# One register load at the entry to the expert loop, and another running order of the experts

## The reference

```python
logits = t @ w_router + b_router             # 256 tokens, 32 experts
top_val, top_idx = lax.top_k(logits, 4)      # four experts for each token
gate_w = softmax(top_val)
# for every expert e, on the tokens that chose it:
hb = xb @ w_exp_in[e] + b_exp_in[e]          # 1024 -> 2048
g = minimum(hb[:, :1024], 7.0); u = clip(hb[:, 1024:], -7.0, 7.0)
a = g * sigmoid(1.702 * g) * (u + 1.0)
y = a @ w_exp_out[e] + b_exp_out[e]          # 1024 -> 1024
# out[token] = sum over its four experts of gate * y, then a residual and a layer norm
```

## Time and profile before

| | us |
|---|---|
| median of 3 runs | 1500.67 (1499.29 to 1502.35) |
| profiled execution, its own time | 1501.61 |
| its span in the trace | 1499.7 |
| TensorE matmul busy | 1336.8 (89%) |
| VectorE, ScalarE, GpSimd busy | 449.4, 359.7, 139.4 |
| data moved | 494.37 MB, mean 330 GB/s over the span |

### The profile page before, as it was taken

The page is one execution under the profiler, slowest core; times in us unless marked ns, Lnnn a source line. Parts: engine busy times, 40 slices in busy tenths (PEclk is TensorE's granted clock), DMA queues, the critical chain, the costliest instruction groups (busy, mean ns, idle before and its releaser), DMA issues.

```text
span 1499.7 us, 25549 instructions
## 1 busy us (share of the span) xinstructions
PE 1336.8 (89%) x9369; PEld 800.7 (53%) x9370; DVE 449.4 (30%) x910; ACT 359.7 (24%) x691; POOL 139.4 (9%) x65
## 2 busy tenths in 40 slices
PE   7999999998999999779998888988879988889965
PEld 6455999987989854334343333343433434333432
DVE  1326687745543871111111111111111111111112
ACT  1234666545566521000000100010010001000101
POOL 0000112005766400000000000000000000000000
PEclk9999999999999999899999999999999999999997
DMA  9441466855344569989999999999999999999996
GB/s 340 149 137 56 112 187 190 322 192 192 134 152 169 184 285 426 406 355 425 428 427 424 428 427 427 423 427 427 427 424 427 427 425 426 428 427 425 422 427 249
DMA packets 113494, 494.37 MB, mean 330 GB/s; under 512 B 7617, under 2 KB 55089, under 8 KB 80465
## 3 DMA queue, kind: packets, MB, share of 16 engines
q1 hardware_dynamic: 111971, 491.50, 81.5%
q10 hardware_dynamic: 1486, 2.34, 0.4%
HBM read 492.76 MB, written 1.06 MB: 329 GB/s over the span
## 4 chain that ended last, share of the span: by engine, by line
PE 63%; DMA 27%; issue 4%; DVE 3%; ACT 3%; SPq 0%; DVEq 0%; ACTq 0%
DMA big_mem<-in_w_exp_in 25%; PE ps L983 17%; PE ps L1025 7%; PE ps L703 5%; PE ps L705 5%; PE ps L704 5%; PE ps L531 4%; PE ps L966 4%; PE ps L675 2%; DMA big_mem<-in_w_exp_out 2%; PE ps L727 1%; PE ps L728 1%; PE ps L729 1%; PE ps L1048 1%; PE ps L1039 1%
## 5 line engine op out<-in xcount | busy, mean ns | idle before, releaser
L983 PE MATMUL ps<-big_mem,ring_mem 128*32 128x512 f32 (+1 forms) x2304 | 373.3, 623 | 54.8 <-DMA big_mem<-in_w_exp_in 54.7
L983 PEld LDWEIGHTS ps<-big_mem,ring_mem 128*32 128x32 f32 (+1 forms) x2304 | 112.5, 122 | 292.9 <-issue 198.7
L1025 PE MATMUL ps<-big_mem,x 128*32 128x256 f32 (+1 forms) x1888 | 186.6, 438 | 5.2 <-ACT x L1596 3.3
L703 PE MATMUL ps<-hT_hi,w_hi 128*128 128x256 f32 x600 | 171.1, 285 | 1.3 <-DVE hT_lo L1683 1.3
L705 PE MATMUL ps<-hT_hi,w_lo 128*128 128x256 f32 x600 | 169.8, 283 | 0.0
L704 PE MATMUL ps<-hT_lo,w_hi 128*128 128x256 f32 x600 | 169.7, 283 | 0.0
L966 PEld LDWEIGHTS ps<-ring_mem,h 128*128 128x128 f32 x1024 | 132.8, 199 | 61.0 <-issue 61.0
L966 PE MATMUL ps<-ring_mem,h 128*128 128x96 f32 x1024 | 150.1, 290 | 0.0
L2169 DVE TENSOR_SCALAR ring_mem<-ps 128x256 f32<-128x256 f32 (+1 forms) x36 | 18.7, 520 | 413.3 <-PE ps L983 413.3
L1583 ACT ACTIVATE ring_mem<-ring_mem 128x256 f32<-128x256 f32 (+1 forms) x36 | 17.7, 493 | 479.6 <-DVE ring_mem L2169 479.6
L1025 PEld LDWEIGHTS ps<-big_mem,x 128*32 128x32 f32 (+1 forms) x1888 | 72.1, 117 | 105.9 <-issue 69.0
(11 more groups left out here) (347 smaller groups left out, 1495.7 us busy)
## 6 DMA issues: line engine op xcount, KB each, us to landing
big_mem<-in_w_exp_in SPq DMA_DIRECT2D x128, 2048.0 KB, 21.2
big_mem<-in_w_exp_out SPq DMA_DIRECT2D x128, 1024.0 KB, 20.8
ring_mem<-in_w_in SPq DMA_DIRECT2D x15, 2048.0 KB, 8.0
ring_mem<-in_w_up SPq DMA_DIRECT2D x44, 512.0 KB, 4.8
ring_mem<-in_w_down SPq DMA_DIRECT2D x5, 2048.0 KB, 8.5
ring_mem<-in_w_out SPq DMA_DIRECT2D x4, 2048.0 KB, 8.4
ring_mem<-in_w_branch_a SPq DMA_DIRECT2D x1, 2048.0 KB, 7.7
ring_mem<-in_w_branch_b SPq DMA_DIRECT2D x1, 2048.0 KB, 7.4
```

Source lines behind the costliest of these rows:

```text
L703: mm(out, hi, x_hi, start=start, stop=False)
L983: last = mm(out, stationary, weights[:, f, w * q:w * (q + 1)] if m > XS else weights[:, :, w * q:w * (q + 1)], start=start, stop=stop)
L1025: last = mm(ps[m * q:m * (q + 1), 4 + at // XS, 0:w], aT[:, k % n, k // n, :], wout[:, k, w * q:w * (q + 1)], start=(k == 0), stop=(k == K ...
```

## The change

Four edits:

1. TensorE: the two products that count tokens go from between the gather's halves to directly behind the rank products; the filler of 512 columns becomes one of 256.
2. TensorE: `counts_ready` is waited for, and the first value of `further` loaded, ahead of the wait for the gates and their transpose. The second value isn't loaded but set to 0; it is loaded only when the first pass outside the loop wasn't taken.
3. VectorE: `own` for expert 0 is made before the residual, `pos` directly behind `further` and ahead of the gates.
4. The table: places 2 and 3 get the ranks 29 and 28 (after 31 and 30 at places 0 and 1), and the remaining 28 places a spread with step 23 modulo 28 in place of step 13 modulo 30.

```diff
-    stay[:, RANKS:RANKS + 2] = E - 1, E - 2
-    stay[:, RANKS + 2:RANKS + E] = 13 * (np.arange(E - 2)[None, :] + 26) % (E - 2)
+    stay[:, RANKS:RANKS + 4] = E - 1, E - 2, E - 3, E - 4
+    stay[:, RANKS + 4:RANKS + E] = 23 * (np.arange(E - 4)[None, :] + 26) % (E - 4)
...
             mm(ps[:, 5, E:2 * E], tri, sel[:, 1, :], start=False, stop=True).then_inc(s["rank_ps"], 1)
-            keep_busy(1, 7)
+            mm(ps[:, 4, 0:E], ones, sel[:, 0, :], start=True, stop=False)
+            mm(ps[:, 4, 0:E], ones, sel[:, 1, :], start=False, stop=True).then_inc(s["rank_ps"], 1)
+            mm(ps[:, 7, 0:SEQ], ident, stay[:, 0:SEQ], start=True, stop=True)
...
                 else:
-                    mm(ps[:, 4, 0:E], ones, sel[:, 0, :], start=True, stop=False)
-                    mm(ps[:, 4, 0:E], ones, sel[:, 1, :], start=False, stop=True).then_inc(s["rank_ps"], 1)
                     pe.wait_ge(s["picks_ready"], 1)
...
+            extra_reg, more_reg, next_extra, next_more = (pe.alloc_register("pe_" + z) for z in ("extra", "more", "next_extra", "next_more"))
+            pe.wait_ge(s["counts_ready"], 1)
+            pe.reg_mov(extra_reg, pe.value_load(further[0:1, 0, 0:1], min_val=0, max_val=TRIO - 1))
+            pe.reg_mov(more_reg, 0)
             pe.wait_ge(s["gates_done"], 1)
             nc.tensor.transpose(ps[0:2 * E, 6, GATE_AT:GATE_AT + P], gate_pair[:], ident).then_inc(s["gateT_ps"], 1)
-            pe.wait_ge(s["counts_ready"], 1)
...
-            pe.reg_mov(extra_reg, pe.value_load(further[0:1, 0, 0:1], min_val=0, max_val=TRIO - 1))
-            pe.reg_mov(more_reg, pe.value_load(further[0:1, 1, 0:1], min_val=0, max_val=PASSES - 1))
...
                 one_pass(GROUPS[1], 16, load_next)
                 turn_end()
+            with pe.If_eq(nth_reg, 0):
+                pe.reg_mov(more_reg, pe.value_load(further[0:1, 1, 0:1], min_val=0, max_val=PASSES - 1))
             with pe.Fori(0, MOST_PASSES):
...
+            dve.wait_ge(s["c_lo_b"], 4)
+            own_row(0, 0)
             dve.wait_ge(s["const_ready"], 1)
...
             v.tensor_copy(further[:], cnt[:]).then_inc(s["counts_ready"], 1)
+            link(v.scalar_tensor_tensor(pos[:], ps[:, 5, 0:T * E].rearrange("p (t e) -> p t e", t=T), 1.0, sel[:], ALU.add, ALU.mult))
             dve.wait_ge(s["own_act"], 3)
```

More of the change, by code:

```diff
@@ L1106, in one_pass @@
                 pe.reg_add(turn_reg, turn_reg, 1)
-            extra_reg, more_reg, next_extra, next_more = (pe.alloc_register("pe_" + z) for z in ("extra", "more", "next_extra", "next_more"))
-            pe.reg_mov(extra_reg, pe.value_load(further[0:1, 0, 0:1], min_val=0, max_val=TRIO - 1))
-            pe.reg_mov(more_reg, pe.value_load(further[0:1, 1, 0:1], min_val=0, max_val=PASSES - 1))
             nth_reg, place_reg, landed_reg, step, step_landed = (pe.alloc_register("pe_" + z) for z in ("nth", "place", "landed", "step", "step_landed"))
@@ L2064, in shifted1, with own_row @@
                 return v.scalar_tensor_tensor(h1[:, t, :], h1[:, t, :], bn[:, 16 * t + 13:16 * t + 14], bc[:, 1, :], ALU.mult, ALU.add)
+            def own_row(e, p):
+                v.tensor_scalar(own, stay[:, bass.ds(OWN + e, 1)].broadcast_to([P, 2 * XS]), 0.0, None, ALU.is_equal).then_inc(s["own_ready"], 1)
+            dve.wait_ge(s["c_lo_b"], 4)
+            own_row(0, 0)
             dve.wait_ge(s["const_ready"], 1)
@@ L2138, in _ @@
             v.memset(posb[:, :, E:E + 1, :], -1.0)
-            link(v.scalar_tensor_tensor(pos[:], ps[:, 5, 0:T * E].rearrange("p (t e) -> p t e", t=T), 1.0, sel[:], ALU.add, ALU.mult))
             link(v.tensor_scalar(posb[:, :, 0:E, 0], pos[:], -1.0, None, ALU.add))
@@ L2176, in swiglu @@
                 v.tensor_tensor(a, u, sig, ALU.mult).then_inc(s["a_ready"], 1)
-            def own_row(e, p):
-                v.tensor_scalar(own, stay[:, bass.ds(OWN + e, 1)].broadcast_to([P, 2 * XS]), 0.0, None, ALU.is_equal).then_inc(s["own_ready"], 1)
             def output(at, m):
@@ L2189, in _ @@
                 dve.reg_mov(r, 0)
-            own_row(0, 0)
             for p in range(1, PASSES):
```

## The result

The changed kernel takes **1515.34 us** (median of 4 runs, 1514.15 to 1515.60) against 1501.51 (1499.29 to 1502.54) for the kernel before on the same chip: ratio 1.0093, 95% interval 1.0075 to 1.011. It is slower, by 14 us where 10 were forecast. The profiled execution took 1515.60 us with a span of 1513.7 (before 1501.61 and 1499.7).

What follows compares the result with a forecast made beforehand. The weight stream's start, holes and short tail were taken to bound the kernel. -4.1 - 7.5 + 20.8 + 1 = +10.2 us on 1500.67 gave 1511 us, range 1504 to 1525.

Steps and rivals of the forecast that it cites:

- What bounds the kernel: Expert part: the DMA weight stream sets the end, through its start, its holes and a short tail; 29.5 us per place.
- Entry, -2.5: Ahead of pass 0: earlier counts and one register load under the gather start pass 0 at 547.9, 2.5 us sooner.
- Clock, -1.6: Pass 0: the shorter gap ahead of it removes TensorE's half-clock stretch, saving 1.6 us, bounds 0 to -1.7.
- first issue: SyncE's first weight transfer for place 1: moves from 556.15 to 552.0, -4.1 us for the whole stream.
- Early holes, -7.5: Stream from 590 to 680 us: light passes at places 2 and 3 close the holes there, -7.5 us.
- Each jump pays: Rival, chance 0.27: ends of places 2 and 3 also pay 7.35 us each, giving 1524 us.
- No second fetch: Rival, chance 0.11: the second code fetch, behind place 4, isn't there; -4.7 us, giving 1506.
- Place 6, hole 8.3: Behind heavy place 6: it starts 16.4 us late, less the 8.1 tolerated, a hole of 8.3 us.
- Places 11, 17 and 28: 2.0, 8.5, 2.0: Behind the other heavy places: holes of 2.0, 8.5 and 2.0 us; place 17 includes 4.9 for the output bias.
- Low clock at places 10 and 27, +1: Middle passes behind light ones, at places 10 and 27: low-clock stretches at times, 1 us added.
- The tail: After the last byte: two light passes, then the norm, the same as before.
- The rule: Heavy passes with a light one behind: 8.1 us late is tolerated; each microsecond beyond is a hole in the stream.

Runs made afterwards that it cites:

- heavy pair: Order with one light place ahead of each heavy one, its heavy expert of place 20 exchanged with the light one of place 14: 1506.81 us.

## Why the prediction was right, and which term was mis-sized

The time was in the range and on the forecast side. Step by step:

- **What bounds the kernel.** Right. From the last landing to the end of the span it is 16.9 us before, 16.4 after, 16.2 with the entry alone and with light places ahead: the time follows the last landing, and that follows the holes. Over all kernels run this tail is 15.1 to 16.9 us, with the same code in it, so differences in time below 2 us between kernels aren't safely those of the holes.
- **Entry, -2.5.** Measured -2.7 (1.40 us from the transpose to pass 0; the forecast had 1.43). The 1.40 is no fixed price behind the transpose, though: with a middle pass at place 3, whose gather has the low stretch, the transpose runs 7.12 us behind the first rank product, 1.5 more than in the changed kernel (5.61), and pass 0 only 0.3 more (7.32 against 7.01). What stands ahead of pass 0 is the sequencer's own chain: the load at 544.57, then register moves up to the branch of L1143 at 546.74.
- **Clock, -1.6.** From the start of pass 0 to the first issue it took 5.83 us and takes 4.16: -1.67. Right here, but not as firm as a single value sounds: with the new table in the old kernel the low stretch there is 6.8 us long, and that distance 6.74 us.
- **Early holes, -7.5.** Measured -6.1 (7.1 to 1.0). The 7.5 were read off the sum of the stretches and all put down to late issues. Only the 5.3 us at place 4 were that (the issue at 653.11). The hole at place 2 is of another kind and stayed (0.7 before, 1.0 now). All its transfers were issued 9.7 us or more before they landed. The fourth quarter of `w_exp_in` landed 5.9 us behind the third in place of 4.9 (599.36 to 605.26), in the stretch that also holds the first long branch and its three instruction packets. It measures 2.1 with the entry alone and 2.0 with two light places ahead. Why the transfer takes longer there isn't shown.
- **Each jump pays (the first rival, 0.27).** Rejected: L1154 is long once in 31, its median 210 ns, though places 2 and 3 took the same jump.
- **No second fetch (0.11).** Rejected: 5.89 us at 681.6, behind place 4 as forecast.
- **Place 6, hole 8.3: the mis-sized term.** It measures **12.9**. Place 5 started 15.3 us late (forecast 14.8), as it should. Pass 5 then took 689.50 to 724.75, 35.25 us, where the forecast had 31 (29.5 and 1.6). So place 6 was 21.0 late, not 16.4, and 21.0 - 8.1 is the hole. The 4.1 us are the clock. Two stretches of the changed kernel's pass 5 (granted clock third from the right):

```profile
688.60:695.40 6.80, 5.90 (x16) 2.10 (x18) 0.00 (x0) 0.00 (x0) 0.00 (x0) 0.50 0.98 407
712.50:715.90 3.40, 3.40 (x10) 0.99 (x10) 0.00 (x0) 0.00 (x0) 0.00 (x0) 0.50 0.97 414
```

The only low stretch of that pass in the kernel with the bias moved, which has the same code and order up to there:

```profile
689.80:693.20 3.40, 2.77 (x10) 1.21 (x12) 0.00 (x0) 0.00 (x0) 0.00 (x0) 0.50 1.00 414
```

9.3 us of busy time at half the clock here, 2.8 there, where the same pass took 31.94 us; 3.1 with the new table in the old kernel, where it took 32.11. Half of 9.3 - 2.8 is 3.25, and the passes differ by 3.3. Half of 9.3 is 4.65, so at full clock this pass would have taken 30.6. The first 5.9 us came directly behind the 5.4 us in which TensorE stood idle for the fetch. The other 3.4 lie 23 us further on, behind gaps of 0.63, 0.47 and 0.24 us that the kernel with the bias moved has as well, without a low stretch: that the fetch caused them isn't shown. The prediction knew of this: the earlier trace rows has a first product of 1.07 us behind the first fetch, and the rival with more fetches carried a low clock. The forecast itself had none behind the second.
- **Places 11, 17 and 28: 2.0, 8.5, 2.0.** Measured 1.8, 9.5, 1.8. Place 17 was 17.6 late, forecast 10.1 + 1.6 + 4.9 = 16.6. All three terms were a little off. The middle pass starts the next one 9.8 late. The second one loses 0.9, not 1.6 (the middle pass of place 22, behind another middle one, takes 30.4 us): the prediction took 3.4 us at half the clock off its 32.7, but that stretch of the kernel before lasts to 615.3, 4.4 us into the pass. The bias adds 5.2 (35.6 against 30.4). Together 15.9, which is what the kernel with a middle pass at place 3 measures. The 1.7 that bring it to 17.6 are the low clock, at place 15.
- **Low clock at places 10 and 27, +1.** Nothing of it is seen there: both heavies behind them are exactly 10.0 late. It fell in place 15, so that place 16 started 11.5 late, where it is 9.8 with the bias moved:

```profile
1012.90:1016.30 3.40, 3.40 (x8) 0.97 (x10) 0.00 (x0) 0.00 (x0) 0.00 (x0) 0.50 0.98 419
```

- **The tail.** 16.4 us from the last byte to the end, 16.9 before.

In all: -4.9 (first issue) - 6.1 + 26.0 = +15.0 for the last landing, which moved by 14.5. The 0.5 between them are small differences in the rate, below what I can assign. The span grew by 14.0 us where 10.2 were forecast. Place 6 alone was 4.6 under, the early holes 1.4 and place 17 1.0. The low-clock term of 1, the first issue (0.8 better than forecast), the two small holes (0.4), the tail and the rate (0.5 each) went the other way. The total is nearer than its largest term, and that much of it is luck.

**The rule holds**: hole = lateness of the heavy pass less 8.1. Over the kernels run, in order of places:

| kernel | lateness of a heavy place | hole behind it |
|---|---|---|
| changed | 21.0, 10.0, 17.6, 10.0 | 12.9, 1.8, 9.5, 1.8 |
| order only | 18.4, 9.9, 17.6, 10.0 | 10.3, 1.9, 10.0, 2.0 |
| bias moved | 17.9, 10.0, 12.6, 9.9 | 9.8, 2.0, 4.5, 1.7 |
| middle at place 3 | 9.9, 11.7, 15.9, 10.0 | 1.8, 3.7, 7.8, 1.9 |
| light ahead | 9.0 (place 6) | 1.1 |
| heavy pair | 8.9 (place 6), 23.1 (place 14) | 2.5, 15.2 |
| heavy at place 2 | 20.1 (place 2) | 13.2 |
| entry only, two light ahead | 8.1 and less | none |

Two of these are off by more than 0.4 us, the first of the heavy pair (2.5 where 0.8 is due) and the one at place 2 (13.2 where 12.0 is due). Both heavy passes began at the low clock, and took 47.3 and 48.1 us instead of 45.8: the 8.1 are for a heavy pass at full clock. With the 1.5 and 2.3 us more of these passes 2.3 and 14.3 are due. At place 2 the slow transfer of that place took 1.1 of them, as a hole of its own: 13.2.

## What to carry to other kernels

With one buffer for each piece of a stream, don't ask which pass is long but how late each pass starts against the stream, and how late it may: here 8.1 us for a heavy pass with a light one behind, and one light pass ahead of each heavy one was worth 24 us against the changed kernel at no other edit. Against the order before, which had a light place ahead of each heavy one too, it was 3.2. An order that places the light work where it closes one hole takes it from where it held others closed, so a new order is counted to its end. And where an engine has stood still in the forecast, its next work is costed at the clock of the nearest row behind such a wait.

## What the runs showed of the hardware

- **A jump over code that hasn't run yet.** Some six to seven microseconds each (5.9 to 7.6) in the long branches of the kernels above, with the DMA queues full of weights, and 210 ns in the median afterwards. The queue of instructions moved three packets around each long one, as in the earlier trace rows. The changed kernel's, from 594 to 608 and from 674 to 694 us:

```profile
q8 instruction: 3, 0.05, 1.8%
...
q8 instruction: 3, 0.05, 1.0%
```

The Trainium skill ("Runtime: NRT & Kernel Launch", Instruction fetch mechanics) has a taken branch to a target that isn't in the window wait for a DMA fetch of it. These rows agree with that, and show in addition that the target isn't fetched again once the code between has run: from 700 to 1490 us no packet of that queue stands in the changed kernel's trace. What decides it exactly stays open: in the kernel with the heavy pass at place 2, the jump over the middle body, not run in the loop by then, took 406 ns; it followed the one long branch (7.0 us from 595.4) at 604.1.
- **The clock behind a wait varies from one kernel to the next.** Pass 5, behind the fetch, had 9.3 us at 1.2 GHz in one kernel (5.9 of them directly behind the wait) and 2.8 in another that had the same code up to there. At the entry the kernel before and the one with the order alone, whose code there is the same, had 3.4 and 6.8 us of it. That is a spread of up to 3 us in the time for which I found no cause in the program.
- **The sequencer runs ahead of its queue.** A register load behind a product that waits in a busy queue begins before that product does (546.3 against 547.51), so its cost is what outlasts the queue.
